# Differential attention scores issued map by map, and the modulation vectors loaded in another order

## The reference, cut to what matters

```python
sh1, sc1, gt1, sh2, sc2, gt2 = jnp.split((jax.nn.silu(c) @ w_mod[i] + b_mod[i])[:, None, :], 6, axis=-1)
csh1, csc1, cgt1, csh2, csc2, cgt2 = jnp.split(jax.nn.silu(c_ctx) @ w_mod[i] + b_mod[i], 6, axis=-1)
```

```python
for blk in range(s // Q_BLOCK):
    q0, q1 = blk * Q_BLOCK, (blk + 1) * Q_BLOCK
    sc = jnp.einsum('bqhmd,bkhmd->bhmqk', q[:, q0:q1], k[:, :q1]).astype(jnp.float32)
    mask = (jnp.arange(q1) // CHUNK_2)[None, :] <= (jnp.arange(q0, q1) // CHUNK_2)[:, None]
    p = jax.nn.softmax(jnp.where(mask, sc, NEG_INF), axis=-1)
    w = p[:, :, 0] - lam * p[:, :, 1]
    outs.append(jnp.einsum('bhqk,bkhd->bqhd', w.astype(v.dtype), v[:, :q1]))
```

## Time and profile before

| | |
|---|---|
| three runs | 5381.85, 5389.64 and 5392.05 us (median 5389.64) |
| the profiled execution: time, span | 5381.96 us, 5379.8 us |
| mean granted clock of TensorE | 0.886 of full |
| TensorE / VectorE / ScalarE busy | 77% / 48% / 31% of the span |
| modulation stage | 4.5 to about 93 us |
| differential attention | first product at 3681.9 us, last exponentials at 3954.6 us |

### The profile page before, as it was taken

One profiled execution on the slowest core, in us unless ns is written; L12 is line 12 of the kernel. 1 busy time (PEld: TensorE's weight loads), 2 busy tenths in 40 slices (PEclk: granted clock), 3 DMA queues, 4 the chain that ended last, 5 costly groups with the idle time before them and its releaser, 6 DMA issues. The chain is left out here.

```text
span 5379.8 us, 73242 instructions
## 1 busy us (share of the span) xinstructions
PE 4132.7 (77%) x29105; PEld 2868.8 (53%) x29105; DVE 2557.6 (48%) x3932; ACT 1687.2 (31%) x3120; POOL 409.5 (8%) x317
## 2 busy tenths in 40 slices
PE   3799954124888572999957999696779887499995
PEld 1688844013888431676636644385644444266663
DVE  2311157675666436665633265424630134366664
ACT  1211022232555311444422144313630022144442
POOL 0000011011000300000000032000000000100001
PEclk7899977566999786999978999898989988699998
DMA  6222111486332332999962322122112221499997
GB/s 232 76 88 80 67 68 47 78 134 132 80 80 76 122 121 87 371 368 365 364 229 91 126 99 71 68 90 91 46 57 70 82 67 69 172 373 384 383 383 288
DMA packets 454569, 844.30 MB, mean 157 GB/s; under 512 B 77552, under 2 KB 277328, under 8 KB 451080
## 3 DMA queue, kind: packets, MB, share of 16 engines
q1 hardware_dynamic: 435448, 785.58, 42.6%
q0 software_dynamic: 12032, 41.96, 2.5%
q10 hardware_dynamic: 6800, 12.71, 0.7%
HBM read 675.72 MB, written 164.45 MB: 156 GB/s over the span
## 5 line engine op out<-in xcount | busy, mean ns | idle before, releaser
L395 PE MATMUL psum<-proj_hi,proj_w 128*128 128x512 f32 (+2 forms) x1728 | 461.2, 356 | 34.9 <-DVE proj_lo L461 34.9
L395 PEld LDWEIGHTS psum<-proj_hi,proj_w 128*128 128x128 f32 (+1 forms) x1728 | 305.4, 189 | 82.7 <-issue 35.1
L2380 PE MATMUL psum<-qkv_w,hT 128*128 128x512 f32 x768 | 334.6, 595 | 12.6 <-DMA qkv_w<-in_w_in 12.6
L2172 ACT ACTIVATE moe_hi<-moe_raw 128x2048 fp32r<-128x2048 f32 x128 | 245.1, 1917 | 301.2 <-PE psum L2123 248.2
L2207 DVE TENSOR_TENSOR moe_lo<-moe_raw,moe_hi 128x2048 fp32r<-128x2048 f32 x128 | 291.7, 2289 | 87.8 <-ACT moe_hi L2172 85.8
L395 PE MATMUL psum<-proj_lo,proj_w 128*128 128x512 f32 (+2 forms) x864 | 306.8, 355 | 0.0
L3748 DVE TENSOR_TENSOR moe_lo<-moe_raw,moe_hi 128x2048 fp32r<-128x2048 f32 x128 | 287.1, 2285 | 33.9 <-ACT moe_hi L3714 33.8
L3714 ACT ACTIVATE moe_hi<-moe_raw 128x2048 fp32r<-128x2048 f32 x128 | 238.5, 1906 | 28.5 <-DMA moe_raw<-in_w_gate_up 28.5
L2380 PEld LDWEIGHTS psum<-qkv_w,hT 128*128 128x128 f32 x768 | 145.4, 191 | 189.1 <-issue 175.9
L2968 PE MATMUL psum<-branches_T,mixed_w 128*128 128x512 f32 x512 | 222.0, 597 | 14.1 <-DMA mixed_w<-in_w_attn_o 14.1
L2133 PE MATMUL psum<-moe_wd,moe_hidT 128*128 128x512 f32 x512 | 225.0, 598 | 8.2 <-DVE moe_hidT L2228 8.2
(11 more groups left out here) (599 smaller groups left out, 8613.2 us busy)
## 6 DMA issues: line engine op xcount, KB each, us to landing
moe_raw<-in_w_gate_up SPq DMA_DIRECT2D x128, 1024.0 KB, 16.9
moe_raw<-in_w_gate SPq DMA_DIRECT2D x64, 1024.0 KB, 7.2
moe_raw<-in_w_up SPq DMA_DIRECT2D x64, 1024.0 KB, 7.4
moe_wd<-in_w_down SPq DMA_DIRECT2D x64, 1024.0 KB, 9.6
moe_wd<-in_w_down SPq DMA_DIRECT2D x32, 2048.0 KB, 11.7
mod_w<-in_w_mod SPq DMA_DIRECT2D x24, 1024.0 KB, 13.1
uT<-proj_out SPq DMA_DIRECT2D x35, 640.0 KB, 2.9
prim<-prep_out SPq DMA_DIRECT2D x32, 640.0 KB, 6.3
```

The source lines that it names most:

```text
L395: last = nc.tensor.matmul(bank[e * nch + c][0:width[e], 0:n], l, r, start=(k == 0 and i == 0), stop=(k == KD - 1 and i == 2))
L2172: nc.scalar.activation(hi[:, n % R], raw[:, n % R], ACT.Copy).then_inc(s["hi_ready"], 1)
L2380: last = nc.tensor.matmul(bank[2 * (n % 2) + c_][:, :], hT[:, k, i * P:(i + 1) * P], w[:, m % 2, k, c_ * BANK:(c_ + 1) * BANK], start=(k = ...
```

## The change

It has two parts that have nothing to do with each other.

In `diff_attention`, `scores` writes map 0's products and its mask behind the wait for map 0's exponentials, and then map 1's products and its mask behind the wait for map 1's. In `maxima` nothing moves: the function became `maximum(j, m)` and is called for both maps at the same places.

In the modulation, the host joins `c` and `c_ctx` into one array `cvec` in the layout of the tile (16 numbers of a partition behind one another), loaded by one transfer. The block ahead of the stage is gone: ScalarE's queue issues the two tables behind `cvec`. The SiLU stands before the 40 issues of bias and gains instead of behind them.

```diff
 def modulation(...)
             @block.scalar
             def _(act):
-                with nc.allow_non_contiguous_dma("vectors as columns"):
-                    act.dma_start(cc[:, :, 0], c.rearrange("o (k p) -> p (o k)", p=P)).then_inc(c_in, 16)
-                    act.dma_start(cc[:, :, 1], c_ctx.rearrange("(k p) -> p k", p=P)).then_inc(c_in, 16)
+                act.dma_start(cc[:, :, :], cvec).then_inc(c_in, 16)
+                for dst, src in tables:
+                    act.dma_start(dst, src).then_inc(tables_in, 16)
+                act.wait_ge(c_in, 16)
+                nc.scalar.activation(sc[:, :, :], cc[:, :, :], ACT.Silu).then_inc(silu, 1)
                 for j in range(COLT):
...
-                act.wait_ge(c_in, 32)
-                nc.scalar.activation(sc[:, :, :], cc[:, :, :], ACT.Silu).then_inc(silu, 1)
...
                 act.wait_ge(out, 16 * stores)
+                act.wait_ge(tables_in, 16 * len(tables))
...
 def diff_attention(...), TensorE
                     free = j - 2 if 1 <= i < 4 else j - 1
-                    if free >= 0:
-                        pe.wait_ge(s["exp"], 2 * free + 2)
-                    for a, b in scores_of(j):
-                        for m in range(2):
-                            z = at(j, m)
-                            nc.tensor.matmul(psum[:, z + a:z + b], q[half[m], h % 2, i * P:(i + 1) * P], k[half[m], h % 2, a:b],
-                                             start=True, stop=False, skip_group_check=True)
+
+                    def products(m, a, b):
+                        z = at(j, m)
+                        nc.tensor.matmul(psum[:, z + a:z + b], q[half[m], h % 2, i * P:(i + 1) * P], k[half[m], h % 2, a:b],
+                                         start=True, stop=False, skip_group_check=True)
+
+                    def mask(m):
+                        z = at(j, m) + i * P + CHUNK2
+                        nc.tensor.matmul(psum[:, z:z + CHUNK2], hide[half[m], :], every[half[m], :], start=False, stop=True,
+                                         skip_group_check=True).then_inc(s_mm[m], 1)
+
                     if j == 0:
                         pe.wait_ge(s["hidden"], 3)
                     for m in range(2):
-                        z = at(j, m) + i * P + CHUNK2
-                        nc.tensor.matmul(psum[:, z:z + CHUNK2], hide[half[m], :], every[half[m], :], start=False, stop=True,
-                                         skip_group_check=True).then_inc(s_mm[m], 1)
+                        if free >= 0:
+                            pe.wait_ge(s["exp"], 2 * free + m + 1)
+                        for a, b in scores_of(j):
+                            products(m, a, b)
+                        mask(m)
...
 def program(...)
-    with nc.Block() as block:
-        @block.sync
-        def _(sp):
-            sp.dma_start(cst[:, :], tabs["cst"]).then_inc(tables_in, 16)
-            sp.dma_start(col[:, :], tabs["cols"]).then_inc(tables_in, 16)
-            sp.wait_ge(tables_in, 32)
-
-    modulation(nc, bank, x["w_mod"], x["b_mod"], x["c"], x["c_ctx"], x["norm_gains"], mod)
+    modulation(nc, bank, x["w_mod"], x["b_mod"], tabs["cvec"], x["norm_gains"], mod,
+               [(cst[:, :], tabs["cst"]), (col[:, :], tabs["cols"])])
```

More of the change, by code:

```diff
@@ L109, in __call__, with modulation @@
         return self.n
-def modulation(nc, bank, w_mod, b_mod, c, c_ctx, gains, mod):
+def modulation(nc, bank, w_mod, b_mod, cvec, gains, mod, tables):
     N = 6 * D
@@ L128, in modulation @@
         o = st.sb("o", [P, SETS, BANK])
+        tables_in = st.sem("tables_in")
         c_in, b_in, gain_in, w_in = st.sem("c_in"), st.sem("b_in"), st.sem("gain_in"), [st.sem(f"w_in{i}") for i in range(R)]
@@ L2850, in wait, with maximum @@
                     dve.wait_ge(s["chain"], n)
-                def maxima(j):
+                def maximum(j, m):
                     n = (j % NT + 1) * P
[L2854 to L2857, removed]
+                    dve.wait_ge(s_mm[m], j + 1)
+                    nc.vector.tensor_reduce(nmax[:, j, m:m + 1], psum[:, at(j, m):at(j, m) + n], AX_X, ALU.max, negate=True)\
+                        .then_inc(s["nm"], 1)
                 def weights(j):
@@ L2903, in _ @@
                     if early and j < J:
-                        maxima(j)
+                        maximum(j, 0)
+                        maximum(j, 1)
                     if 1 <= j <= J:
@@ L3845, in program @@
     bank = [psum[:, i * BANK:(i + 1) * BANK] for i in range(8)]
-    tables_in = nc.alloc_semaphore("tables_in")
     def scratch(name, *shape, dt=F32):
@@ L4063, in columns @@
             pc[p, :, PCOL["w0"] + d] = v[:, COLS["w0"] + 4 * d + p]
-    return dict(cols=v, pcols=pc)
-WHOLE = ("x", "c", "ctx", "c_ctx", "w_mod", "b_mod", "norm_gains", "w_in", "rwkv_w2", "rwkv_a2", "rwkv_g2",
+    both = np.stack([np.asarray(x["c"], np.float32).reshape(D), np.asarray(x["c_ctx"], np.float32).reshape(D)])
+    return dict(cols=v, pcols=pc, cvec=both.reshape(2, KD, P).transpose(2, 1, 0))
+WHOLE = ("x", "ctx", "w_mod", "b_mod", "norm_gains", "w_in", "rwkv_w2", "rwkv_a2", "rwkv_g2",
          "w_out", "w_router", "w_gate", "w_up", "w_down", "mem_2", "positions_2", "q_norm_2", "k_norm_2", "w_in_2",
```

## The result

The changed kernel takes 5406.14 us (median of 12 runs) against 5392.05 us for the kernel before (12 runs). The ratio is 1.0027, 95% interval 1.0016 to 1.0038, so it is 9 to 20 us slower. The forecast was 5361 us and faster. The profiled execution has a span of 5400.9 us against 5379.8, 21.1 us longer, and the two parts of the change account for nearly all of it: the modulation ends 13.5 us earlier, and the attention takes 33.8 us longer, 20.3 us in all.

A forecast was written before the change was run, and what follows sets the result against it. Nothing global decides: the weight stream sets the modulation's end, a chain of exponentials, scores and maxima the attention's wide tiles. Gains of 15 + 13 = 28 us, from the median 5389.6, give 5361 us, range 5343 to 5378.

The forecast's parts named there:

- the term of 12.9 us for the attention's release: Attention tiles i = 7, 6, 5: VectorE's idle time ahead of the maxima goes, gaining 12.9 us, bounds 0 and 23.
- the overlap between the maps: Attention scores: products of the two maps still overlap when written apart, partially, starting after the first product.
- Rival 2: Attention gains nothing: map 1's scores come late or TensorE gets the lower clock more often; 5375 us, chance 0.17.
- Modulation, 15 us: Modulation: closing the hole in the weight stream gives 12.7 us, the earlier front 2.2; bounds 11 to 17.
- near bound of 3.0: Modulation: cvec lands in 3.0 us, as cst did on an empty queue; the far bound is c_ctx's 18.2 us.
- Rival 3: Modulation: cvec lands late, some 4 us of the stream's hole remain; 5365 to 5366 us, chance 0.12.
- Tile 4 gains nothing: Attention, i = 4: none of VectorE's 10.4 us idle counted, since earlier release doesn't help or the clock is low.
- Rival 4: Attention: wide tiles i = 4 gain too, up to 10 us more; 5351 us, chance 0.08.
- rival 1: Attention scores: the maps run one behind the other, costing 26 us in all; slower, 5401 us, chance 0.08.
- If a later stage changes its length, the argument that barriers pass the gain on is wrong.: Stages after the attention: they should keep their length, so that earlier gains reach the program's end.

The follow-up runs named there:

- wide5: Third run: the changed kernel with only tiles i = 5, 6, 7 map by map, tiles 0 to 4 in turn as before; 5363.39 us, 0.9945 of the kernel before.
- fill: Fifth run: the changed kernel with unread extra products in TensorE's idle stretches ahead of tiles 2 and 4; 5352.93 us, 0.9927 of the kernel before.
- wide5_fill: Map by map for tiles 5, 6, 7 alone, plus unread filling products in TensorE's idle stretches, against the changed kernel; 5357.88 us, 0.9928 of the kernel before.
- runs 1 to 4: Against the kernel before: modulation part alone 0.999; attention part alone 1.0041; both, map by map only in tiles 5 to 7, 0.9945, or only 0 to 4, 0.9988.
- run 5: The changed kernel with unread extra products in TensorE's idle stretches ahead of tiles 2 and 4; 5352.93 us, 0.9927 of the kernel before.
- run 7: The changed kernel with one unread product beside map 0's first, in wide tiles of three heads; 5388.49 us, 0.9988 of the kernel before.
- Run 8: The changed kernel with the filling products issued from the lower 64 partitions alone; 5363.72 us, 0.9926 of the kernel before.
- run 9: The changed kernel with only the idle stretch ahead of tile 2's transposes filled; 5373.49 us, 0.9947 of the kernel before.
- half: Seventh run: the changed kernel with one unread product beside map 0's first, in wide tiles of three heads; 5388.49 us, 0.9988 of the kernel before.

## Why the prediction was wrong

**The step that failed** is the term of 12.9 us for the attention's release. It takes for granted, with no reason given, that the new order is granted the clock of the old one. The stage was at the lower level for 121 us instead of 38 and took 33.8 us more, where the term has 12.9 less. "I take it as holding" was said of the overlap between the maps, which did hold, in part; of the clock nothing was said there. Rival 2 named the lower clock but let it cost no more than the gain, "the attention gains nothing", 5375 us, and the range was drawn from that price. The rows had the warning in them: rows 8 show a wide tile at a granted clock of 0.50 in the old order (TensorE had been idle for 2.52 us before it). I took that as a reason to count no gain for tile 4. I did not ask what the new order would do to a tile that starts at that clock, where it makes the scores 4.6 us long and TensorE the bound.

Point by point:

- *Modulation, 15 us.* Right in mechanism, 13.5 us measured in the stage and inside the bounds of 11 to 17. `cvec` landed in 5.4 us, between the near bound of 3.0 and the far one, and the hole went all the same. Rival 3 did not come.
- *The attention's release, 12.9 us.* Right where the clock is the same: 32.1 to 30.5 us in a head at clock 1.00. Times 8 that would be 12.8, but only such heads show it. `wide5`, where only the three tiles of the term are changed and the granted clock of the stretch is about that of before (0.94, 0.93), gained 11.2 us. With filling in both orders the gain of these three tiles is 19.4 us (267.3 to 247.9); how much of that is the clock (0.96 to 0.99) no run tells.
- *Tile 4 gains nothing.* It held. `wide5_fill` leaves tile 4 in the old order and needs 247.9 us, `fill` releases it map by map and needs 249.8. Rival 4 did not come.
- *The overlap across maps.* Right, and partial, as the prediction said. In narrow tiles both maps run as pairs, though map 0's mask now stands between them in the program; four passes of 384 columns take the 0.92 us that they took before, and the first mask starts only at 3718.27:

```profile
3717.52 0.92 PE L2742 MATMUL psum<-attn_k,attn_q 64*128 64x384 f32 x4
```

  In the wide tile i = 7 above, six passes start ahead of map 0's mask, and map 0 has only four. The other two of map 1 start at 3739.73, behind it. The prediction named products of map 1 behind map 0's mask as the sign of rival 1. So half of that sign is there, and at the upper clock it cost nothing.
- *Rival 1, 5401 us, maps one behind the other.* Its time is close to the measured 5406, and its mechanism happened only in part, without its price: with the clock held (`fill`), the same order is 18.2 us faster than the old. A time that fits is not a mechanism that is shown. The rule from the Trainium skill ("TensorE: Matmul & The Clock Gate", Part 3 on packing small matmuls), that matmuls start strictly in program order, is contradicted here by the row above as by rows 9.
- *"If a later stage changes its length, the argument that barriers pass the gain on is wrong."* It stands: from the last exponentials to the end of the program, the two profiles have 5379.8 - 3954.6 = 1425.2 us and 5400.9 - 3975.6 = 1425.3 us.

What is shown is that the order of the scores decides the clock in this stage (runs 1 to 4), that this clock is what costs (run 5), and that one more product beside map 0's, or filled gaps, gives it back (runs 5 and 7). That the working half of the array is what matters is the reading that fits run 7 best, and it is not shown. Run 8 bounds it: in the short gaps of the second to the eighth head half an array held the clock as well as a whole one. What starts a fall stays open (run 9).

## What to carry to other kernels

Products in different halves of the partitions that run as pairs save TensorE's time, and in this stage they also kept its clock. Before drawing such pairs apart to release another engine earlier, look for rows with a granted clock of 0.50 in the stage, and cost the new order at that clock as well, from the row. If TensorE then becomes the bound, the loss can be larger than the gain: here 33.8 us, where 12.9 were to be gained. Draw apart only the tiles whose wait is worth it (`wide5`), or give TensorE something to do in the gaps (`fill`). And a transfer or an activation on which a stream depends belongs ahead of the issues that it doesn't need.

## What the runs showed of the hardware that was not expected

- TensorE was busier by its records and had a lower clock. The attention shows it busy for 279.6 of 301.8 us at 0.80, where the old order has 206.7 of 268.0 us at 0.93. Between 3878.00 and 3886.00 us of the changed kernel it is busy without a gap, and the clock stays at the lower level:

```profile
3878.00:3886.00 8.00, 8.00 (x27) 5.82 (x27) 3.43 (x6) 3.57 (x9) 0.00 (x0) 0.50 0.00 1
```

- More work made the program faster: twelve added products of 512 columns in `half` shortened the attention from 301.8 to 285.3 us.
- The stage's clock is repeatable. Two orders and four start times gave 268.0, 267.9, 301.8 and 301.7 us.
